# Down projection of a two-block transformer kernel: seven block products for 7 of 22 k pairs, and an alternating order of passes in the channel units

## The reference, cut to what matters

```
h = rmsnorm(x, g_ffn)                                   # 256 x 2048
u = causal_dwconv(h @ w_up, ffn_conv_w) + ffn_conv_b    # 256 x 11264, 3 taps over tokens
gate, val = split(u, 2)                                 # 256 x 5632 each
x = x + (silu(gate) * val) @ w_down                     # w_down: 5632 x 2048
out = rmsnorm(x, g_final)
```

## Time and profile before

| | us |
|---|---|
| median of 3 runs | 1965.17 |
| lowest and highest | 1964.43, 1965.48 |
| profiled execution | 1964.4 |
| its span | 1962.6 |
| TensorE busy | 1944.7 (99%) |
| VectorE busy | 1289.4 (66%) |
| ScalarE busy | 1028.8 (52%) |
| DMA, mean | 182 GB/s |
| granted TensorE clock, mean | 0.999 of 2.4 GHz |

### The profile page before, as it was taken

One profiled execution on the slowest core, in us unless ns is written; L12 is line 12 of the kernel. 1 busy time (PEld: TensorE's weight loads), 2 busy tenths in 40 slices (PEclk: granted clock), 3 DMA queues, 4 the chain that ended last, 5 costly groups with the idle time before them and its releaser, 6 DMA issues.

```text
span 1962.6 us, 28709 instructions
## 1 busy us (share of the span) xinstructions
PE 1944.7 (99%) x9868; PEld 1645.5 (84%) x9868; DVE 1289.4 (66%) x1806; ACT 1028.8 (52%) x1503; POOL 47.1 (2%) x74
## 2 busy tenths in 40 slices
PE   8999999999999999999999999999999999999998
PEld 7788888888888888888888888888888888888886
DVE  6655675656655676655768765778778787754444
ACT  5533576664433576654544444555555555544443
POOL 1000030000000020000100000000000000000000
PEclk9999999999999999999999999999999999999999
DMA  8666445545566545545666445556555565565553
GB/s 297 202 194 192 143 157 154 160 151 186 182 195 193 147 161 172 155 155 181 209 193 190 154 168 186 181 183 192 184 190 190 184 192 184 191 214 193 194 193 139
DMA packets 246726, 357.29 MB, mean 182 GB/s; under 512 B 15303, under 2 KB 136481, under 8 KB 246109
## 3 DMA queue, kind: packets, MB, share of 16 engines
q1 hardware_dynamic: 245004, 349.35, 55.8%
q0 software_dynamic: 1616, 6.61, 1.0%
HBM read 352.75 MB, written 3.16 MB: 181 GB/s over the span
## 4 chain that ended last, share of the span: by engine, by line
PE 96%; DVE 1%; ACT 1%; issue 1%; DMA 1%; SPq 0%; DVEq 0%; ACTq 0%
PE acc L368 21%; PE acc L345 19%; PE acc L347 19%; PE acc L346 19%; PE acc L361 11%; PE aux L425 2%; PE aux L833 1%; DVE sb_w_lo L308 1%; PE aux L851 1%; PE aux L850 1%; PE aux L814 1%; DMA sb_stage<-w_kv 0%; PE aux L820 0%; PE aux L822 0%; PE aux L821 0%
## 5 line engine op out<-in xcount | busy, mean ns | idle before, releaser
L308 DVE TENSOR_TENSOR sb_w_lo<-sb_stage,sb_w_hi 128x1024 fp32r<-128x1024 f32 x652 | 799.4, 1228 | 513.8 <-ACT sb_w_hi L303 506.9
L303 ACT ACTIVATE sb_w_hi<-sb_stage 128x1024 fp32r<-128x1024 f32 x652 | 688.7, 1059 | 640.4 <-PE acc L347 372.0
L368 PE MATMUL acc<-sb_xT,sb_w_hi 128*128 128x512 f32 x1856 | 455.3, 392 | 0.0
L368 PEld LDWEIGHTS acc<-sb_xT,sb_w_hi 128*128 128x128 f32 x1856 | 337.6, 189 | 62.6
L345 PE MATMUL acc<-sb_w_hi,sb_xT 128*128 128x512 f32 x768 | 306.6, 399 | 0.4 <-issue 0.4
L347 PE MATMUL acc<-sb_w_hi,sb_xT 128*128 128x512 f32 x768 | 299.8, 390 | 0.0
L346 PE MATMUL acc<-sb_w_lo,sb_xT 128*128 128x512 f32 x768 | 299.6, 390 | 0.0
L361 PEld LDWEIGHTS acc<-sb_xT,sb_w_lo 128*128 128x128 f32 x1856 | 245.6, 191 | 13.3
L361 PE MATMUL acc<-sb_xT,sb_w_lo 128*128 128x256 f32 x1856 | 252.3, 284 | 0.0
L345 PE MATMUL acc<-sb_w_hi,sb_mT 128*128 128x512 f32 x560 | 224.9, 402 | 1.6 <-issue 1.0
L347 PE MATMUL acc<-sb_w_hi,sb_mT 128*128 128x512 f32 x560 | 218.8, 391 | 0.0
(11 more groups left out here) (255 smaller groups left out, 1472.0 us busy)
## 6 DMA issues: line engine op xcount, KB each, us to landing
sb_stage<-w_in SPq DMA_DIRECT2D x248, 512.0 KB, 3.9
sb_stage<-w_up SPq DMA_DIRECT2D x176, 512.0 KB, 3.4
sb_stage<-w_out SPq DMA_DIRECT2D x96, 512.0 KB, 3.5
sb_stage<-w_down SPq DMA_DIRECT2D x88, 512.0 KB, 4.3
sb_stage<-w_kv SPq DMA_DIRECT2D x16, 512.0 KB, 6.8
sb_stage<-w_ukv SPq DMA_DIRECT2D x16, 512.0 KB, 3.4
sb_stage<-w_uq SPq DMA_DIRECT2D x12, 512.0 KB, 3.5
sb_kz<-mem SPq DMA_DIRECT2D x8, 256.0 KB, 7.2
```

What stands on the lines that cost most here:

```text
L303: act.activation(w_hi[:, j % RING, 0:size], stage[:, j % RING, 0:size], ACT.Copy).then_inc(hi_ready, 1)
L308: dve.tensor_tensor(w_lo[:, j % RING, 0:size], stage[:, j % RING, 0:size], w_hi[:, j % RING, 0:size].bitcast(F32), ALU.subtract).then_inc( ...
L368: mm = pe.matmul(acc[:, 2 * pair + c, :], hi[:, k, c * P:(c + 1) * P], both, start=first and k == 0, stop=last and k == 3)
```

## The change

A product of a 2 x 2 block matrix by a 2 x 2 block matrix takes 8 block products, or 7 with sums of blocks before and after (Strassen's scheme in Winograd's form). Here the blocks are: two token tiles by two k tiles of the activations, and two k tiles by two column blocks of 512 of `w_down`. The change uses the seven products for k pairs 0 to 6, the eight for pairs 7 to 21.

- **Activations.** In turns 1 to 7 of the up projection `ffn_act` also makes four sums of 128-token blocks (`ffn_sevens`) and writes hi and lo of three of them to a new tile `seven_T`; the fourth takes the place of one block in `act_T`.
- **Weights.** The four blocks of a pair go by two loads into one of two `pair_stage` buffers. They become four units of the ring: `seven0` (two blocks as loaded), `seven1` (one block), then four sums on VectorE, then `seven2` and `seven3` (two blocks each). `pair_stage` and two further ring slots (`down_hi`, `down_lo`; the ring has six now) lie in the memory of `xT`, the activations of the up projection.
- **Order.** The columns are done in two chunks of 1024; within a chunk row units of both column blocks and the sevens are interleaved. There are 116 units, and preparation runs five ahead (`prepared_at`).
- **Banks.** Of a chunk's seven products three accumulate into `acc` banks with the row units, four into the `aux` banks. After the last seven of a chunk ScalarE copies one bank, and VectorE makes eight additions (`add_sevens`) into x, four at each of two units.
- **Channel units.** Every second unit does the long passes first.

```diff
-            if first:
+            if (k0 // 4) % 2 == 0:
                 main_passes()
                 mm = rest_passes()
...
+SEVEN = 7
+DOWN_PAIRS = [[[7, 8], 0, [9, 10], 1, [11, 12], 2, [13, 14], 3, [15, 16], 4, [17, 18], 5, [19], 6, [20, 21]],
+              [[7, 8], 0, [9, 10], 1, [11, 12], 2, [13, 14], 3, [15], 4, [16], 5, [17], 6, [18, 19, 20, 21]]]
...
+                units += [("rows", k, 2 * chunk + half) for half in range(2) for k in item]
...
+                units += [(f"seven{part}", item, chunk) for part in range(4)]
...
+def prepared_at(u):
+
+    ahead = {0: [3], 1: [4], 2: [5], 3: [6, 7], 4: [8, 9]}.get(u, [u + 5])
+    return [j for j in ahead if j < U_DOWN]
...
+        def rest_down(step, dve, j):
+
+
+            dve.wait_ge(hi_ready, U4 + (j + 1))
+            src, hi, lo = down_parts(j)
+            dve.tensor_tensor(lo, src, hi.bitcast(F32), ALU.subtract).then_inc(lo_ready, 1)
+            if DOWN[j][0] == "seven1":
...
+                dve.wait_ge(lo_ready, U4 + (j + 1))
+                step(dve.tensor_tensor(b11, b11, b12, ALU.add))
+                dve.tensor_tensor(b12, b12, b22, ALU.add).then_inc(sums_ready, 1)
+                dve.wait_ge(sums_ready, 2 * sevens_until(j) - 1)
+                step(dve.tensor_tensor(b22, b11, b22, ALU.add))
+                dve.tensor_tensor(b21, b22, b21, ALU.add).then_inc(sums_ready, 1)
...
+                def load_pair(n):
+
+                    _, i, chunk = DOWN[SEVEN_FIRST[n]]
+                    if n < 2:
+                        sp.wait_ge(unit_used, U4)
+                    else:
+                        sp.wait_ge(lo_ready, U4 + (SEVEN_FIRST[n - 2] + 4))
...
+                for r, j in enumerate(DOWN_ROWS):
+                    load_row_unit(r)
+                    if r == 3:
+                        load_pair(0)
+                    for n, first in enumerate(SEVEN_FIRST[:-1]):
+                        if first + 4 == j:
+                            load_pair(n + 1)
...
+                    pe.wait_ge(lo_ready, U4 + (j + 1))
+                    passes(m_first, near(0, 0), j, 0, first, last)
+                    passes(acc[:, 2, :], mixed(2), j, 1).then_inc(unit_used, 1)
+                    pe.wait_ge(lo_ready, U4 + (j + 2))
+                    passes(acc[:, 0, :], near(1, 0), j + 1, 0).then_inc(unit_used, 1)
+                    pe.wait_ge(lo_ready, U4 + (j + 3))
+                    passes(m_fifth, mixed(0), j + 2, 0, first, last)
+                    passes(m_seventh, near(0, 1), j + 2, 1, first, last).then_inc(unit_used, 1)
+                    pe.wait_ge(lo_ready, U4 + (j + 4))
+                    passes(m_sixth, mixed(1), j + 3, 0, first, last)
+                    passes(acc[:, 1, :], near(1, 1), j + 3, 1).then_inc(unit_used, 1)
...
+                for j in range(U_DOWN):
+                    for ahead in prepared_at(j):
+                        round_down(act, ahead)
+                    if j == 0:
+                        copy_value(N_FFN)
+                    if j == 1:
+                        tap2(N_FFN, 1, 1)
+                    if j - 1 in SEVEN_END:
+                        multiplied(act, U4, j - 1)
+                        act.activation(first_f, m_first, ACT.Copy).then_inc(first_copied, 1)
...
+                    step(dve.tensor_tensor(first, a21, a22, ALU.subtract))
+                    step(dve.tensor_tensor(second, a11, first, ALU.subtract))
+                    step(dve.tensor_tensor(fourth, a12, second, ALU.subtract))
+                    step(dve.tensor_tensor(a21, a11, a21, ALU.subtract))
...
+                for j in range(U_DOWN):
+                    for ahead in prepared_at(j):
+                        rest_down(step, dve, ahead)
+                    if j == 0:
+                        ffn_sums(N_FFN, 1, 1)
+                    if j == 1:
+                        ffn_conv(N_FFN, 1, 1)
+                    if j == 2:
+                        ffn_act(N_FFN, 1)
...
-    nc = _bacc.Bacc("TRN2", target_bir_lowering=False, num_devices=1)
+    nc = _bacc.Bacc("TRN2", target_bir_lowering=False, num_devices=1, dynamic_dma_scratch_size=2048)
```

More of the change, by code:

```diff
@@ L126, with down_units, sevens_until @@
 OUT_PAIRS = [0, 1, 2, 6, 7, 3, 4, 5]
+SEVEN = 7
+DOWN_PAIRS = [[[7, 8], 0, [9, 10], 1, [11, 12], 2, [13, 14], 3, [15, 16], 4, [17, 18], 5, [19], 6, [20, 21]],
+              [[7, 8], 0, [9, 10], 1, [11, 12], 2, [13, 14], 3, [15], 4, [16], 5, [17], 6, [18, 19, 20, 21]]]
+def down_units():
+    units = []
+    for chunk, items in enumerate(DOWN_PAIRS):
+        for item in items:
+            if isinstance(item, list):
+                units += [("rows", k, 2 * chunk + half) for half in range(2) for k in item]
+            else:
+                units += [(f"seven{part}", item, chunk) for part in range(4)]
+    return units
+DOWN = down_units()
+U_DOWN = len(DOWN)
+DOWN_END = [max(j for j, unit in enumerate(DOWN) if unit[0] == "rows" and unit[2] == c) for c in range(4)]
+SEVEN_END = [max(j for j, unit in enumerate(DOWN) if unit[0] == "seven3" and unit[2] == chunk) for chunk in range(2)]
+DOWN_TAIL = U_DOWN - 4
+DOWN_ROWS = [j for j, unit in enumerate(DOWN) if unit[0] == "rows"]
+SEVEN_FIRST = [j for j, unit in enumerate(DOWN) if unit[0] == "seven0"]
+DOWN_RING = 6
+def sevens_until(j):
+    return sum(first <= j for first in SEVEN_FIRST)
+def prepared_at(u):
+    ahead = {0: [3], 1: [4], 2: [5], 3: [6, 7], 4: [8, 9]}.get(u, [u + 5])
+    return [j for j in ahead if j < U_DOWN]
 POOL_PIECES = [[(0, 0, 128), (1, 0, 64)], [(1, 64, 64), (2, 0, 128)],
@@ L1111, in _, with passes @@
                     ffn_turn(turn_)
[L1113 to L1118, removed]
+                def passes(o, a, j, part, start=False, stop=False):
+                    hi, lo = (ap[:, part * 512:(part + 1) * 512] for ap in down_slot(j))
+                    pe.matmul(o, a(0), hi, start=start, stop=False)
+                    pe.matmul(o, a(0), lo, start=False, stop=False)
+                    return pe.matmul(o, a(1), hi, start=False, stop=stop)
@@ new lines, in product_down, with product_seven @@
+                def product_down(j, first, last):
+                    _, i, c = DOWN[j]
+                    pe.wait_ge(lo_ready, U4 + (j + 1))
+                    for k in range(2):
+                        for t in range(T):
+                            mm = passes(acc[:, 2 * (c % 2) + t, :], lambda h: act_T[:, 2 * i + k, h, t * P:(t + 1) * P], j, k,
+                                        first and k == 0, last and k == 1)
+                    mm.then_inc(unit_used, 1)
+                def product_seven(j, first, last):
+                    _, i, _ = DOWN[j]
+                    near = lambda k, t: lambda h: act_T[:, 2 * i + k, h, t * P:(t + 1) * P]
+                    mixed = lambda n: lambda h: seven_T[:, i, h, n * P:(n + 1) * P]
+                    pe.wait_ge(lo_ready, U4 + (j + 1))
+                    passes(m_first, near(0, 0), j, 0, first, last)
[8 more added lines that the diff above has]
+                    passes(acc[:, 1, :], near(1, 1), j + 3, 1).then_inc(unit_used, 1)
@@ new lines, in _ @@
+                for j, (kind, i, c) in enumerate(DOWN[:DOWN_TAIL]):
+                    if c == 0:
+                        pe.wait_ge(act_ready, i + 1)
+                    if kind == "rows":
+                        first = j == min(r for r in DOWN_ROWS if DOWN[r][2] == c)
+                        if first:
+                            banks_free(pe, PAIRS4, c)
+                        product_down(j, first, j == DOWN_END[c])
+                    if kind == "seven0":
+                        if j == SEVEN_FIRST[SEVEN]:
+                            pe.wait_ge(seven_free, 1)
+                        product_seven(j, j in (SEVEN_FIRST[0], SEVEN_FIRST[SEVEN]), j + 3 == SEVEN_END[c])
```

158 lines of the change are left out of this document (112 added, 46 removed).

## The result

The changed kernel takes 1967.6 us, median of 20 runs (1964.77 to 1969.42), against 1964.25 for the kernel before in 20 runs (1963.85 to 1965.91). The ratio is 1.0014 with a 95% interval of 1.0008 to 1.0021: slightly slower, where 1957.9 and faster was forecast. The profiled execution has a span of 1965.8 us, 3.2 more than before.

A forecast was written before the change was run, and what follows sets the result against it. TensorE was taken as the bound, with 96% of the last chain. 1964.4 - 9.5 - 1.2 + 3.4 = 1957.1 us for the profiled execution, 1957.9 as the median; range 1953.8 to 1963.0.

The forecast's parts named there:

- (d): First seven of the down projection: pair 0 lands at 5.3 us, TensorE idles 3.4 us before part 2.
- (f): Between the chunks: 1.6 us of VectorE room left, cost taken as 0, bounds 0 and 2; the ending stays.
- (a): Down projection: 42 fewer matmuls at an unchanged pace of 0.2267 us, saving 9.5 us.
- (e): The other thirteen sevens: 3.8 us left in a dense place, cost taken as 0, far end 38 us.
- (b): Channel units' alternating pass order in the up projection: saves 1.2 us, bounds 0 and 2.3.
- (c): VectorE's extra 2.9 us in each of seven up projection turns: cost taken as 0, far end 20 us.
- rival (3): Pair 0 shares the rate with loads behind it, landing at 10, stall of 8 us: 1962.5; chance 0.14.
- Rival (4): The clock falls in the first seven's stall, losing half the stall's time, 1.7 us: 1959.6; chance 0.07.
- (g): Cut descriptor space for GpSimd's loads: cost taken as 0, bounds 0 and 3 us.
- (2): Rival: next to no stall at the first seven, 1 us: 1955.5; chance 0.08.

The follow-up runs named there:

- the last run: Kernel with the three edits of order and six row units ahead of the first seven, plus row units 4 and 5 loaded before pair 0: 1954.58 us.
- the new order alone: The kernel before with only the alternating order of long and short passes in the channel units: 1963.54 us, ratio 0.9996.
- run with the hold: Changed kernel, but the sync engine waits for both loads of pair 0 to land before issuing the next load: 1965.06 us.
- the filled hole: Changed kernel with 18 matmuls of unused result before the wait for part 2 of the first seven: 1964.41 us.
- the run with the last turn's work first: Changed kernel, but the last up turn's scaling, convolution and gate product come before part 0's rounding and rest: 1962.09 us.

## Why the prediction was wrong

The saving came and the price of it was mis-sized. Three terms failed: in (d) the landing of pair 0, taken at 5.3 us and measured at 7.9 (2.4 us more of hole); the clock behind the holes, put at nothing and measured at 4.6; and (f), put at nothing and measured at 2.6 between the chunks and 0.8 at the end. Together they are the 10.4 us between -7.3 and +3.1.

- **(a), (e)** hold. With every hole removed the stage takes what 42 fewer matmuls give, thirteen sevens in dense and loose places included.
- **(b)** holds as a pace: 0.84 us over 42 periods, so 1.2 over 58. That the down stage started just 1.20 sooner was luck. Its start differs by 1.4 us between traces with the same order of passes, alone the order gives 0.9 in the medians, within the interval, and the last run, with every hole removed, is 9.6 below before and not 10.7.
- **(c)** holds. With the sevens' sums in seven turns, the up projection takes the same 469.44 us from 1243.13 on as with the new order alone.
- **(d)** is right in place, order and releaser, and mis-sized: "I take 5.3" stands for a landing of pair 0 that came at 7.9 us. Put into the forecast's own chain, 7.9 gives a start of part 2 at 18.7 after the release; it was 1731.34 - 1712.75 = 18.6. The far end of the range given there, 7.0, was too low as well. The wrong inference was that loads behind pair 0 don't slow it because they landed in order at the kernel's start: order of landing says nothing of the rate. The run with the hold shows 1.4 us between the two. That is a small part of rival (3), which had them share the rate in full and land at 10. The Trainium skill, "DMA: Bandwidth & Descriptors", section "Queues, rings and completion order", says that each DMA engine consumes descriptors in ring order. The loads land in their order here too, but the rule doesn't say that the first ones land as if alone.
- **Rival (4)**, given 0.07, is what happened, on top of the longer hole: 2.9 us by the profile, 3.2 by the filled hole. The sum had put this term at nothing. The rival's price of half the stall was close in this trace (2.9 for 5.0 us, 1.7 for 2.6). In the traces of the experiments it wasn't steady: 1.5 and 1.7 for 5.0, 1.5 for 4.4, 1.6 for 3.0, 1.7 for one hole of 2.3, and nothing for two others of 2.3 and for holes of 2.7, 2.2 and 1.9. The Trainium skill, "TensorE: Matmul & The Clock Gate", section "HAM oscillation", by which waits between groups of matmuls throttle the engine, was right where the sum was not.
- **(f)** is the step that failed in kind. It summed VectorE's work over eight row units and found 1.6 us to spare (its 12.6 us of rests and sums come to 11.7 by the prices of (e), so the surplus was, if anything, larger), but left out two things: the row loads have four stage slots for a ring of six, so VectorE idled 2.3 us for one in this very stretch, and what TensorE waits for first is the bank of block 0, behind eight additions in VectorE's order, not the next unit's data. A sum over the stretch hides both. The ending's 4.5 us against 5.4 assumed that VectorE comes to the block's sum in time; it came 2.4 us late, behind the late additions and the rest of the last unit.
- **(g)** shows nothing in the trace: `kvb` is used from 63.10 us, 63.11 before. No run tests it alone.
- The low end of the range, (2) with 2.3 for (b) and no stall, comes to 1953.4 and not 1953.8. It changes nothing.

So in the profiled execution a gain of 10.7 us, the 1.2 of (b) partly by luck, stood against 13.8 us given back at two places and the ending. The last run shows that order alone gives them back, but for 0.2 us at the ending.

## What to carry to other kernels

When a kernel is bound by one engine throughout, price a change's waits one by one in program order, for every resource that is released (data, bank, stage slot), because a surplus summed over a stretch doesn't protect the first use in it. A hole on TensorE can cost more than its length: the clock behind one took up to 2.9 us more here, not in every execution. Filling the hole with work that computes nothing gave back the clock's part, 3.2 us in the medians, and nothing of the hole itself; only an earlier release or useful work that is ready does that. Loads issued in a burst after a release land late as a group: put what can be loaded before the release ahead of it.

## What the runs showed of the hardware that was not expected

- Two loads of 512 KB into an idle queue land 5.2 and 6.1 us after their issue, not 3.4 to 4.5 as single ones do; with six more issued behind them by 1718.0 us, 5.8 and 7.5, and the third 8.3.
- The granted clock can fall after TensorE has already gone on: in the second hole TensorE idled for 2.6 us at 1.00, resumed at 1838.87 with starts 0.23 to 0.33 us apart, and only from 1839.67 ran at 0.43 a matmul.
- Whether the clock falls differs between holes of the same length: behind 2.3 us it cost 1.7 us at the second hole of the run with the last turn's work first, and nothing at that run's first hole.
- The pace of 0.2267 us for 128x512 passes is the same in the kernel before, which sums in two banks at a time with all weights in `w_hi` and `w_lo`, and in the last run (229.62 us for 1013 starts), which sums in all eight and takes operands from `down_hi`, `down_lo` and `seven_T` too.
